# Feed-forward up and gate products with the weights stationary from the second step on

## The reference

```python
def rms_norm(x, g):
    x32 = x.astype(jnp.float32)
    y = x32 * lax.rsqrt(jnp.mean(x32 * x32, axis=-1, keepdims=True) + EPS)
    return (y * g.astype(jnp.float32)).astype(x.dtype)

def swiglu(h, w1, w3, w2):
    return (jax.nn.silu(h @ w1) * (h @ w3)) @ w2

h = rms_norm(x, norm_ffn_g[layer])
x = x + swiglu(h, ffn_w1[layer], ffn_w3[layer], ffn_w2[layer])
```

## Time and profile before

| | |
|---|---|
| median of 3 runs | 1005.72 us |
| profiled execution, first to last instruction | 1004.0 us |
| TensorE busy with matmuls | 985.5 us (98%), 4760 matmuls |
| weight loads (beside the matmuls) | 811.2 us |
| VectorE busy | 570.9 us (57%) |
| ScalarE busy | 475.9 us (47%) |
| mean granted TensorE clock | 1.000 |
| bytes read from HBM | 175.98 MB |

### The profile page before, as it was taken

How to read it: one execution, slowest core, us unless ns; L and a number is a source line. 1 busy time by engine, 2 the same in 40 slices (tenths; PEclk the granted TensorE clock), 3 DMA queues, 4 the chain that set the end, 5 groups by cost and what they waited for, 6 DMA issues and landing times.

```text
span 1004.0 us, 12665 instructions
## 1 busy us (share of the span) xinstructions
PE 985.5 (98%) x4760; PEld 811.2 (81%) x4760; DVE 570.9 (57%) x630; ACT 475.9 (47%) x519; POOL 44.0 (4%) x59
## 2 busy tenths in 40 slices
PE   6999999999999999999999999999999999999998
PEld 5777888888888888888888888778888888888887
DVE  5777645454474756754544475773465675454443
ACT  5446534343455664644444455455444354444442
POOL 3230000000000000000000012000000000000000
PEclk9999999999999999999999999999999999999999
DMA  8723755565555333655555555445435456555641
GB/s 278 270 98 113 262 172 204 169 206 171 204 188 171 126 126 126 201 197 179 197 177 197 177 189 203 142 145 182 161 128 207 153 187 206 171 205 169 207 167 42
DMA packets 112311, 177.57 MB, mean 177 GB/s; under 512 B 6801, under 2 KB 74513, under 8 KB 112273
## 3 DMA queue, kind: packets, MB, share of 16 engines
q1 hardware_dynamic: 110704, 172.53, 50.7%
q0 software_dynamic: 1280, 3.94, 1.2%
q10 hardware_dynamic: 288, 0.59, 0.2%
HBM read 175.98 MB, written 1.05 MB: 176 GB/s over the span
## 4 chain that ended last, share of the span: by engine, by line
PE 92%; DVE 3%; DMA 2%; POOL 1%; ACT 1%; issue 1%; ACTq 0%; DVEq 0%; POOLq 0%
PE psum L1311 28%; PE psum L1313 28%; PE psum L1312 28%; PE psum L1375 4%; DMA poolw<-in_ev_pool_w 1%; DVE arena L1102 1%; PE psum L1625 1%; DMA cst<-consts 1%; DVE small L1101 1%; POOL head_rs L528 1%; PE psum L1646 1%; PE psum L1408 1%; PE psum L1395 1%; DVE low L907 0%; PE psum L1427 0%
## 5 line engine op out<-in xcount | busy, mean ns | idle before, releaser
L907 DVE TENSOR_TENSOR low<-raw,high 128x2048 fp32r<-128x2048 f32 (+1 forms) x161 | 365.1, 2268 | 300.1 <-ACT high L583 299.7
L583 ACT ACTIVATE high<-raw 128x2048 fp32r<-128x2048 f32 (+1 forms) x163 | 309.1, 1896 | 258.7 <-PE psum L1313 257.3
L1311 PE MATMUL psum<-high,xh 128*128 128x512 f32 x912 | 361.7, 397 | 1.3 <-DVE low L907 1.3
L1313 PE MATMUL psum<-high,xl 128*128 128x512 f32 x912 | 355.9, 390 | 0.0
L1312 PE MATMUL psum<-low,xh 128*128 128x512 f32 x912 | 355.3, 390 | 0.0
L1313 PEld LDWEIGHTS psum<-high,xl 128*128 128x128 f32 x912 | 171.2, 188 | 36.5
L1311 PEld LDWEIGHTS psum<-high,xh 128*128 128x128 f32 x912 | 171.3, 188 | 36.2 <-DVE low L907 1.5
L1312 PEld LDWEIGHTS psum<-low,xh 128*128 128x128 f32 x912 | 171.5, 188 | 33.7
L1311 PE MATMUL psum<-high,gh 128*128 128x512 f32 x240 | 93.6, 390 | 0.0
L1313 PE MATMUL psum<-high,gl 128*128 128x512 f32 x240 | 93.4, 389 | 0.0
L1312 PE MATMUL psum<-low,gh 128*128 128x512 f32 x240 | 93.4, 389 | 0.0
(11 more groups left out here) (147 smaller groups left out, 621.1 us busy)
## 6 DMA issues: line engine op xcount, KB each, us to landing
raw<-in_ffn_w SPq DMA_DIRECT2D x132, 512.0 KB, 4.3
raw<-in_w_in SPq DMA_DIRECT2D x52, 512.0 KB, 4.5
raw<-in_od_w_qkv SPq DMA_DIRECT2D x24, 512.0 KB, 4.5
raw<-in_w_ffn_gate SPq DMA_DIRECT2D x22, 512.0 KB, 3.7
raw<-in_w_ffn_up SPq DMA_DIRECT2D x22, 512.0 KB, 4.7
raw<-in_w_ffn_down SPq DMA_DIRECT2D x22, 512.0 KB, 3.9
raw<-in_ev_w_in SPq DMA_DIRECT2D x12, 512.0 KB, 5.9
raw<-in_ev_w_out SPq DMA_DIRECT2D x8, 512.0 KB, 4.4
```

Of the source, the lines that this page charges most:

```text
L583: nc.scalar.activation(high[:, n % RING, 0:cols], raw[:, n % RING, 0:cols], ACT.Copy).then_inc(high_ready, 1)
L907: nc.vector.tensor_tensor(low[:, n % RING, 0:cols], raw[:, n % RING, 0:cols], high[:, n % RING, 0:cols].bitcast(F32), ALU.subtract).then_i ...
L1311: nc.tensor.matmul(out, sh, wh, start=start, stop=False, skip_group_check=True)
L1313: return nc.tensor.matmul(out, sl, wh, start=False, stop=stop, skip_group_check=True)
```

## The change

From step 1 on the up and gate products are turned round. The 128x128 weight tiles are stationary, and x is streamed. `xh` and `xl` become two halves of one tensor `xhl`, so one matmul streams both (512 columns: wh with xh and wh with xl, in two halves of one bank), and a second matmul streams `xh` alone under the low weights (256 columns, added to the first half). There are four banks for 2 x 128 gate columns (0, 1) and 2 x 128 up columns (6, 7). The result has hidden columns on the partitions and tokens along the free axis, which is what the down product needs, and the transposes of the gated tile are left out from step 1 on. Step 0 stays as it was, with its transposes now in bank 2.

The two halves of a bank have to be added: ScalarE copies the second half out, VectorE adds it to the first. The factor 1/rms now varies along the free axis. It is made into a row, the same on all partitions, once per feed-forward (`rstd_columns` on VectorE, two transposes on TensorE, a copy on ScalarE), and VectorE multiplies gate and up with it. SiLU and the product of gate and up run from SBUF to SBUF, and `gh`, `gl` are made from SBUF.

```diff
+GATE_BANK, UP_BANK = 0, 6
+HT_BANK, RSTD_BANK = 2, 3
...
-        xh = sb("xh", [P, KD, SEQ], F32R)
-        xl = sb("xl", [P, KD, SEQ], F32R)
+        xhl = sb("xhl", [P, KD, 2 * SEQ], F32R)
+        xh, xl = xhl[:, :, 0:SEQ], xhl[:, :, SEQ:2 * SEQ]
...
 # ScalarE
+                def gated(c, i):
+                    act.wait_ge(gateT_done, turned(f, c) + 1)
+                    nc.scalar.activation(f_gateT_lo, halves(GATE_BANK)[1], ACT.Copy).then_inc(gate_lo_ready, 1)
+                    act.wait_ge(gate_scaled, turned(f, c) + 1)
+                    nc.scalar.activation(f_gateT, f_gateT, ACT.Silu).then_inc(siluT_ready, 1)
+                    act.wait_ge(unit_used, n0 + 4 + 3 * i)
+                    nc.scalar.activation(f_upT_lo, halves(UP_BANK)[1], ACT.Copy).then_inc(up_lo_ready, 1)
...
                 def step(c, i):
                     split_high(n0 + 4, i)
-                    split_high(n0 + 5, i)
-                    hiddenT(c - 1)
-                    gated(c)
+                    if isinstance(c, int) and c == 1:
+                        split_high(n0 + 5, i)
+                        hidden_first()
+                        rstd_row()
+                    else:
+                        hidden_high(c - 1)
+                        split_high(n0 + 5, i)
+                    gated(c, i)
                     split_high(n0 + 6, i)
...
 # VectorE
+                def gate(c):
+                    dve.wait_ge(gate_lo_ready, turned(f, c) + 1)
+                    nc.vector.tensor_tensor(f_gateT, halves(GATE_BANK)[0], f_gateT_lo, ALU.add).then_inc(gate_sum, 1)
+                    dve.wait_ge(gate_sum, turned(f, c) + 1)
+                    nc.vector.tensor_tensor(f_gateT, f_gateT, rrow, ALU.mult).then_inc(gate_scaled, 1)
+                def up(c):
+                    dve.wait_ge(up_lo_ready, turned(f, c) + 1)
+                    nc.vector.tensor_tensor(f_upT, halves(UP_BANK)[0], f_upT_lo, ALU.add).then_inc(up_sum, 1)
+                    dve.wait_ge(up_sum, turned(f, c) + 1)
+                    nc.vector.tensor_tensor(f_upT, f_upT, rrow, ALU.mult).then_inc(up_scaled, 1)
+                    dve.wait_ge(up_scaled, turned(f, c) + 1)
+                    dve.wait_ge(siluT_ready, turned(f, c) + 1)
+                    nc.vector.tensor_tensor(f_upT, f_upT, f_gateT, ALU.mult).then_inc(gatedT_ready, 1)
...
                 def step(c, i):
                     split_low(n0 + 4, i)
-                    split_low(n0 + 5, i)
-                    hiddenT(c - 1)
-                    gated(c)
-                    if isinstance(c, int) and c == FSTEPS - 1:
-                        hiddenT(c)
+                    if isinstance(c, int) and c == 1:
+                        split_low(n0 + 5, i)
+                        hidden_first()
+                        dve.wait_ge(rrow_copied, f + 1)
+                    else:
+                        hidden_low(c - 1)
+                    last = isinstance(c, int) and c == FSTEPS - 1
+                    if not last and not (isinstance(c, int) and c == 1):
+                        split_low(n0 + 5, i)
+                    gate(c)
+                    up(c)
+                    if last:
+                        hidden_low(c)
+                        split_low(n0 + 5, i)
                     split_low(n0 + 6, i)
...
 # TensorE
+            def turned_unit(n, second, i):
+                pe.wait_ge(low_ready, n + 1 + 3 * i)
+                for b, at in enumerate((GATE_BANK, GATE_BANK + 1, UP_BANK, UP_BANK + 1)):
+                    for k in range(4):
+                        kk = 4 * second + k
+                        c = slice(b * P, (b + 1) * P)
+                        wh, wl = slot_tile(high, n, k, 512)[:, c], slot_tile(low, n, k, 512)[:, c]
+                        nc.tensor.matmul(bank(at), wh, xhl[:, kk, :], start=kk == 0, stop=False, skip_group_check=True)
+                        ins = nc.tensor.matmul(bank(at, 0, SEQ), wl, xh[:, kk, :], start=False, stop=kk == KD - 1,
+                                               skip_group_check=True)
+                    if second and b == 1:
+                        ins.then_inc(gateT_done, 1)
+                ins.then_inc(unit_used, 1)
...
-                def step(c, i, start, mid=None):
+                def step(c, i, start):
                     n = n0 + 2
-                    if not (isinstance(c, int) and c == 1):
-                        pe.wait_ge(hidden_ready, 2 * (FSTEPS * f + c))
-                    wide_unit(n, 0, SET_A, 512, wide_ready[0], i)
-                    hiddenT(c - 1)
-                    wide_unit(n + 1, 1, SET_A, 512, wide_ready[0], i)
-                    down(n + 2, c - 1, start, False, i, mid)
+                    first = isinstance(c, int) and c == 1
+                    if not first:
+                        pe.wait_ge(up_sum, turned(f, c))
+                    turned_unit(n, 0, i)
+                    if first:
+                        hidden_first()
+                        rstd_row()
+                    turned_unit(n + 1, 1, i)
+                    if first:
+                        pe.wait_ge(rrow_copied, f + 1)
+                    down(n + 2, c - 1, start, False, i)
```

More of the change, by code:

```diff
@@ L250, in program @@
         f_silu, f_hidden = blocks(take(NT * FC), NT), blocks(take(NT * FC), NT)
+        f_gateT, f_upT = blocks(take(2 * SEQ), 2), blocks(take(2 * SEQ), 2)
+        f_gateT_lo, f_upT_lo = blocks(take(2 * SEQ), 2), blocks(take(2 * SEQ), 2)
+        f_rcols, f_rrow = blocks(take(NT * P), NT), take(SEQ)
         take = Carve()
@@ L385, in chunk_done, with first_step_done, turned, halves @@
                 before = sum(1 for u, ss, _ in wide_chunks if ss == s and u < unit)
-                steps = (FSTEPS - 1) * sum(1 for u in U_FFN if u < unit) if s == 0 else 0
-                eng.wait_ge(wide_ready[s], before + steps + 1)
-        def step_done(eng, f, c, t):
+                eng.wait_ge(wide_ready[s], before + 1)
+        def first_step_done(eng, f, t):
             if t:
-                eng.wait_ge(unit_used, U_FFN[f] + (3 * c + 1 if c_late(c) else 2))
+                eng.wait_ge(unit_used, U_FFN[f] + 2)
             else:
-                ss = step_set(c)
-                before = sum(1 for u, s, _ in wide_chunks if s == ss and u < U_FFN[f])
-                eng.wait_ge(wide_ready[ss], before + ((FSTEPS - 1) * f + c if c_late(c) else f + 1))
-        def step_set(c):
-            return 0 if c_late(c) else 2
+                eng.wait_ge(wide_ready[2], f + 1)
+        def turned(f, c):
+            return (FSTEPS - 1) * f + c - 1
+        def halves(b):
+            return psum[:, b:b + 2, 0:SEQ], psum[:, b:b + 2, SEQ:2 * SEQ]
         def hidden_tile(first, last, c):
             return last[:, 0:2, :] if isinstance(c, int) and c == FSTEPS - 1 else first[:]
-        def c_late(c):
-            return not isinstance(c, int) or c > 0
         QK_T_BEFORE = {3: (0, 0), 5: (0, 1)}
@@ L678, in hiddenT, with hidden_high @@
+                def hidden_high(c):
+                    act.wait_ge(gatedT_ready, turned(f, c) + 1)
+                    if not (isinstance(c, int) and c == FSTEPS - 1):
                         act.wait_ge(unit_used, n0 + 2 + 3 * c)
-                    nc.scalar.activation(hidden_tile(gh, mh, c), bank(6).rearrange("p (k n) -> p k n", k=2), ACT.Copy).then_inc(gh_ready, 1)
+                    nc.scalar.activation(hidden_tile(gh, mh, c), f_upT, ACT.Copy).then_inc(gh_ready, 1)
                 def step(c, i):
@@ L690, in ffn @@
                 act.wait_ge(rstd_ready, 2 * NORMS.index(FFN_NORM[f]) + 2)
[L691 removed]
+                gated_first()
                 step(1, 0)
@@ L1021, in gated, with rstd_columns @@
                                                        scalar=x_rstd(FFN_NORM[f], t), in1=f_silu[:, t, :],
                                                        op0=ALU.mult, op1=ALU.mult).then_inc(hidden_ready, 1)
-                def hiddenT(c):
+                def rstd_columns():
+                    if f:
+                        dve.wait_ge(rrow_ready, f)
+                    for t in range(NT):
+                        nc.vector.tensor_scalar(f_rcols[:, t, :], ident, 0.0, x_rstd(FFN_NORM[f], t),
+                                                ALU.mult, ALU.add).then_inc(rcols_ready, 1)
@@ L1431, in ffn, with hidden_first @@
             def ffn(f, xk, late=None):
                 n0 = U_FFN[f]
-                def hiddenT(c):
-                    pe.wait_ge(hidden_ready, 2 * (FSTEPS * f + c) + 2)
-                    if f or c_late(c):
-                        pe.wait_ge(gl_ready, FSTEPS * f + c)
-                    transposes(6, [f_hidden[:, t, k * P:(k + 1) * P] for k in range(2) for t in range(NT)], hiddenT_ready)
-                def down(n, c, start, stop, i=0, mid=None, late=None):
+                def hidden_first():
+                    pe.wait_ge(hidden_ready, 2 * f + 2)
```

(8 more changed lines are left out.)

50 lines of the change are left out of this document (31 added, 19 removed).

## The result

The changed kernel takes 1009.58 us (median of 5 runs, 1009.44 to 1010.23) against 1005.72 us for the kernel before (5 runs, 1004.98 to 1005.88). The ratio is 1.004 with a 95% interval of 1.003 to 1.0051: slower by 0.4%, where 0.57% less was forecast. The profiled execution spans 1008.4 us instead of 1004.0, at a granted clock of 1.0 in both.

The account below looks back on a forecast made before the run. TensorE was taken as the bound, its time being instructions times pitch. The terms -14.6 + 3.5 + 0.65 + 3.5 + 1.2 = -5.75 us gave a 998.3 us span and 1000.0 us time, 0.57% less; 8-in-10 range 995.0 to 1005.5.

Parts of the forecast that it names:

- part 2: Turned up and gate products: per step 16 long matmuls fewer, 32 short ones more at 0.117 us each; +3.5 us.
- row of 1/rms: Two more transposes per feed-forward, behind the four that stay, 0.11 us each: +0.65 us.
- What bounds the kernel: In feed-forward steps TensorE never waits; time is its number of instructions times their pitch, busy 985.5 of 1004.0 us.
- Part 1: Transposes of the gated tile go, ten groups fewer in each of three feed-forwards, 30 x 0.49: -14.6 us.
- my upper bound: Short matmul pays the long one's whole excess over streaming its 512 columns: 0.120 us each, 2.9 us more.
- the index product: Existing matmul with 256 columns and 68 weight columns; its 22 pitches gave the 0.117 us taken for short products.
- rival A: Uneven pitch of 0.231 does not settle as matmul kinds alternate: 4.1 us more, 1004.1, perhaps 1005; chance 0.18.
- long ones at 0.231 throughout: Sign of a wrong forecast: 512-column matmuls in turned units at 0.231 us instead of 0.227.
- Rival B: Short matmul is held by its successor's weight load: slower from 0.123 us, 1006 to 1010 or more; chance 0.10.
- Serial loads: Weight loads not hidden at all, 16 more per step at 0.19 us: 91 us more, 1091; 0.01 of Rival B's chance.
- Part 4: VectorE and ScalarE work in loop steps hides behind TensorE, up sum ready with 3.2 us to spare: cost nothing.
- Part 5: Last step of each feed-forward: weight-tile wait 1.15 us, three times, +3.5; late transposes wait 0.6 us, twice, +1.2.

Follow-up runs that it names:

- `before_one_T`: The kernel before, with three of the four transposes of a step left out from step 1 on: 996.16 us beside 1005.84.
- `lastorder`: Changed kernel with the low part of the last down unit's weights made ahead of the gating again: 1005.13 us, ratio to the kernel before 0.9994.
- experiment 6: `grouped_short64`: the kernel with runs of eight, its 256-column products loading and using only 64 weight columns (work left out): 1000.73 us against 1004.48.
- experiment 1: `grouped`: changed kernel issuing eight long products, then eight short ones, instead of one by one: 1004.48 us, ratio to the kernel before 0.9992.
- experiment 2: `short272`: changed kernel with the short product streaming 272 columns instead of 256: 1015.81 us, 6.2 more.
- experiment 3: `long_w64`: changed kernel with the 512-column products using only 64 of 128 weight columns (work left out): 998.35 us, 11.2 less.
- `onerun`: Changed kernel with one run of 32 short products per step and the last weight tile ahead of the gating: 998.88 us, ratio to the kernel before 0.9935.
- `group2`: Changed kernel with runs of two long, then two short products: 1004.69 us against 1009.58.
- `group4`: Changed kernel with runs of four long, then four short products: 1006.10 us against 1009.58.
- `grouped_long64`: The kernel with runs of eight, its 512-column products loading and using only 64 weight columns (work left out): 1004.40 us against 1004.48.
- `short_w64`: Changed kernel with the 256-column products using only 64 of 128 weight columns (work left out): 1002.34 us, 7.2 less.

## Why the prediction was wrong

The sum fails at one term, part 2, the pitch of the 256-column products among the 512-column ones: +3.5 us were forecast, and +12.3 came. The ledger of the spans:

| term | predicted us | measured us | from |
|---|---|---|---|
| transposes gone, 30 groups | -14.6 | -14.6 | not measured as a whole; `before_one_T` gave 9.7 for three of four |
| turned products | +3.5 | +12.3 | 30 x (11.29 - 48 x 0.2267) |
| uneven start of the down units | 0 | +1.8 | 30 x (16.79 - 11.29 - 24 x 0.2267), uncertain by the rounding of the rows |
| row of 1/rms | +0.65 | +0.65 | not measured apart |
| wait in the last steps | +3.5 | +3.6 | 3 x 1.20 |
| late transposes | +1.2 | +0.4 | 2 x 0.2; `lastorder` gave 4.45 for this and the row above |
| sum | -5.75 | +4.15 | spans: 1008.4 - 1004.0 = +4.4 |

The step of 16.79 us in the third term is the distance between the starts of two steps on TensorE in the changed kernel:

```profile
144.71 0.39 PE L1511 MATMUL psum<-xhl,high 128*128 128x512 f32 x1
...
161.50 0.39 PE L1511 MATMUL psum<-xhl,high 128*128 128x512 f32 x1
```

It had been 16.81 before. So the change gained almost nothing in the loop (0.02 us a step, 0.6 us in 30), and what it costs at the ends is the loss.

- **What bounds the kernel**: right. TensorE set the time before and after; but for the waits at the ends, the difference came from its own instructions.
- **Part 1** (-0.49 us per step): right as far as it was checked, by leaving out three of the four transposes.
- **Part 2**: this step failed. Against settled rows of either kind, the 8.8 us missing come in two pieces. 960 x 3 ns = 2.9 us are the settled pitch of a short product: 0.120, not 0.117. That was my upper bound, worked out from the long product's own excess. I preferred the index product, though its weights have 68 columns, and width counts in a row of short products (0.114 us with 64 columns, 0.120 with 128, experiment 6). And the earlier trace rows were one short product whose successor started early; the first short product of each run looks like this, and the long ones behind the run pay it back (experiment 1: 1.84 against 1.81 us). A single distance between two starts is not a pitch.
- The other 5.9 us (6 ns in each of 960 pairs) are the extra of the one-by-one order. It was rival A, which I gave 4.1 us and a chance of 0.18; it is real, larger (6 ns a pair instead of 4.3), and added to the short product's 0.120. The bounds of part 2 had been taken one at a time, and both upper ones came true together: 1000.0 + 2.9 + 4.1 is 1007.0, outside the range. In the changed kernel's own rows the two pieces cannot be told apart: there the short product is followed after 0.117 us on average, just as forecast, and the whole excess stands in the long one's 0.236. The prediction had named long ones at 0.231 throughout as a sign of being wrong; that sign came, at 0.236.
- **The start of the down units** (+1.8 us) had no term in the sum; rival A alone had mentioned it.
- **Rival B** had the right sign and the right warning: break-even at 0.123 for the short product, 6 ns from the forecast. The settled pair was 9.6 ns above the forecast's. Its plain form, a short product that lasts as long as its successor's load, is refuted: streaming 16 more columns cost 6.2 us, and at 2.4 GHz 960 x 16 columns take 6.4 (experiment 2). But the load is not free either: with a load half as wide under each short product the pair lost all of its excess (experiment 3, 0.340). Serial loads did not come about: their 1091 us are far off, and in `onerun` long products keep 0.226 us with loads of 0.19 between them. This is against the rule on row groups of the Trainium skill's page "TensorE: Matmul & The Clock Gate", section "The mechanism". The same section also lets a load run ahead when it goes to the background weight buffer; no run here tells whether that is what happens.
- **Part 4**: right. The up sum ended in time. In the loop of the changed kernel, VectorE's sum and TensorE's next step:

```profile
258.07 0.69 DVE L1080 TENSOR_TENSOR arena<-psum,arena 128x512 f32<-128x512 f32 x1 [1.18 <-ACT arena L698]
...
262.26 0.39 PE L1511 MATMUL psum<-xhl,high 128*128 128x512 f32 x1
```

The sum ends at 258.07 + 0.69 = 258.76 and TensorE begins the next step at 262.26. That is 3.5 us to spare, 3.2 were forecast.
- **Part 5**: right in place and size for the wait (1.20 for 1.15, three times), and too large for the late transposes (0.2 for 0.6): the additions started 1.98 us into the unit and not 2.3.

What stays open is why products issued one by one cost more than the two settled pitches. For the same 32 long and 32 short products a step took:

| order | 32 pairs, us |
|---|---|
| sum of settled pitches, 32 x (0.2267 + 0.1200) | 11.09 |
| one run of 32 (`onerun`) | 11.11 |
| runs of eight (`grouped`) | 11.14 |
| runs of two (`group2`) | 11.13 |
| runs of four (`group4`) | 11.20 |
| one by one (changed kernel) | 11.29 |

That order alone decides 0.18 us per step is shown. The mechanism in the engine is not. The row is not monotonic, and the width of the weights enters in a way that no theory here gives: halving it for long products made the alternating pair faster (0.340, without any extra) and saved nothing in runs of eight. One rival was not separated: an order also sets how soon a bank of PSUM is written again, and in the changed kernel each short product adds to the bank that the long one just before it wrote. Runs of long products write the same bank four times in a row at the settled 0.227, and `long_w64` has the changed kernel's order of banks and no extra, which speaks against it; no run changes the banks alone.

## What to carry to other kernels

Where TensorE is the bound and a change turns matmuls of one shape into more and shorter ones, count each one's excess in full (here 13 ns over the streaming time in settled rows, with 128 weight columns at 512 and at 256 columns alike), and compare with the margin: here 6 ns per short matmul decided. Take a pitch only from a long row of the same shape and the same weight width, and where the margin is that small, take the upper bounds together. If two shapes must be mixed, try them in runs instead of one by one: runs of two gave nearly all of it here, one run of 32 the most. With the same instructions, one long run of short products and a weight tile put back ahead of the gating turned a loss of 0.4% into a gain of 0.65% (10.7 us, of which the tile alone was 4.45).

## What the runs showed of the hardware

- The settled pitches with 128 weight columns are 0.2267 us at 512 and 0.1200 at 256 columns, 13.3 ns over 512/2.4 and 256/2.4 in both cases (`onerun`).
- A run of eight short products with 64 weight columns has 0.114 us each, with 128 0.120; a run of eight long ones behind the down unit 0.230 with 64 columns and 0.227 with 128 (`grouped_short64`, `grouped_long64`, `grouped`).
- Alternating pairs have 0.353 us with 128 weight columns in both, 0.360 with 16 streamed columns more, 0.347 with 64 weight columns in the short one and 0.340 with 64 in the long one (changed kernel, `short272`, `short_w64`, `long_w64`). The sum of the settled pitches with 128 is 0.347.
- A load of 128 weight columns lasts 0.19 us in the trace, one of 64 columns 0.13 (`long_w64`), and both run while matmuls stream.
- The first short product behind a row of long ones is followed after 0.11 us already, and the long ones behind a row of short ones are slower, by 0.03 us for a run of 8 as for one of 32.
